# Per-part dependency buffers and measured step costs in the build-time order of a hybrid attention and gMLP layer

## What is computed

```python
h = x @ W_in + b_in                      # -> q | k | v | z | gate_a | gate_g
y_a = sliding_window_attention(q, k, v, sinks) @ w_br_a
y_g = chunked_spatial_gating(gelu(z), ...) @ w_br_g
mix = sigmoid(gate_a) * y_a + sigmoid(gate_g) * y_g
x = layer_norm(alpha * x + mix @ w_out)
x = layer_norm(alpha * x + relu(x @ w_up)**2 @ w_down)
```

## Time and profile before

| | |
|---|---|
| executions | 1038.11, 1037.97 and 1236.2 us; median 1038.11 us |
| profiled execution | 1037.65 us |
| its span on the slowest core (core 4) | 1036.1 us; cores 1035.0 to 1036.1 us |
| TensorE busy | 1004.8 us, granted clock 0.996 of full |
| VectorE, ScalarE, GpSimd busy | 589.8, 380.6, 101.3 us |
| DMA | 98.85 MB, 95 GB/s |

### The profile page before, as it was taken

How to read it: one execution, slowest core, us unless ns; L and a number is a source line. 1 busy time by engine, 2 the same in 40 slices (tenths; PEclk the granted TensorE clock), 3 DMA queues, 4 the chain that set the end, 5 groups by cost and what they waited for, 6 DMA issues and landing times.

```text
span 1036.1 us, 16955 instructions; the slowest of 8 cores (1035.0 to 1036.1 us)
## 1 busy us (share of the span) xinstructions
PE 1004.8 (97%) x5792; PEld 491.3 (47%) x5902; DVE 589.8 (57%) x1226; ACT 380.6 (37%) x578; POOL 101.3 (10%) x163
## 2 busy tenths in 40 slices
PE   9999999999999999999999999999999999999995
PEld 3446455554444444444444645555444444444442
DVE  3866577765776312444676837777486842134454
ACT  0456566641325200331134645666223430023221
POOL 4210000000111000000023000000010100010015
PEclk9999999999999999999999999999999999999998
DMA  9995243253787902954299222632366564086012
GB/s 163 194 174 97 42 66 58 42 114 84 148 144 147 151 8 44 163 78 83 85 181 149 47 41 42 106 60 42 102 137 128 86 127 73 1 137 107 9 74 82
DMA packets 20630, 98.85 MB, mean 95 GB/s; under 512 B 2369, under 2 KB 3265, under 8 KB 12098
## 3 DMA queue, kind: packets, MB, share of 16 engines
q0 software_dynamic: 13200, 73.14, 45.2%
q1 hardware_dynamic: 7346, 24.61, 7.2%
HBM read 162.50 MB, written 8.39 MB: 165 GB/s over the span
## 4 chain that ended last, share of the span: by engine, by line
PE 90%; DVE 5%; issue 2%; ACT 1%; DVEq 0%; POOL 0%; ACTq 0%; POOLq 0%
PE ps L443 58%; PE ps L1206 21%; PE ps L696 3%; DVE scr L948 2%; PE ps L977 1%; PE ps L936 1%; PE ps L552 1%; ACT regK L415 1%; PE ps L836 1%; PE ps L998 1%; PE ps L1123 1%; PE ps L1029 1%; PE ps L1219 1%; DVE lnbuf L401 1%; DVE scr L404 1%
## 5 line engine op out<-in xcount | busy, mean ns | idle before, releaser
L443 PE MATMUL ps<-reg,ring 128*128 128x512 bf16 x1500 | 340.9, 379 | 2.4 <-issue 0.7
L443 PE MATMUL ps<-xT_s,ring 128*128 128x512 bf16 (+1 forms) x1060 | 245.6, 377 | 5.3 <-DVE den L1012 2.9
L443 PEld LDWEIGHTS ps<-reg,ring 128*128 128x128 bf16 x1536 | 147.4, 98 | 174.7 <-issue 3.9
L1206 PE MATMUL ps<-ring,reg 128*128 128x512 bf16 x972 | 213.7, 379 | 1.1
L415 ACT ACTIVATE scr<-ps 128x512 f32<-128x512 f32 x128 | 76.5, 597 | 262.8 <-PE ps L443 253.6
L443 PEld LDWEIGHTS ps<-xT_s,ring 128*128 128x128 bf16 x1104 | 103.1, 98 | 116.1 <-issue 6.8
L1206 PEld LDWEIGHTS ps<-ring,reg 128*128 128x128 bf16 x992 | 97.1, 98 | 117.0
L404 DVE SCALAR_TENSOR_TENSOR reg<-ps,scr 128x512 bf16<-128x512 f32 x128 | 87.7, 690 | 113.6 <-ACT scr L415 113.4
L948 DVE CUSTOM_DVE_ANT_1 scr<-ps,lnbuf 128x384 f32<-128x384 f32 x128 | 71.1, 555 | 51.2 <-PE ps L936 31.7
L415 ACT ACTIVATE scr<-scr,amx 128x384 bf16<-128x384 f32 x128 | 78.5, 613 | 37.1 <-DVE amx L404 30.0
L471 POOL DMA_DIRECT2D ring<-wst x62 | 34.2, 555 | 446.8 <-PE ps L443 177.3
(11 more groups left out here) (104 smaller groups left out, 824.3 us busy)
## 6 DMA issues: line engine op xcount, KB each, us to landing
ring<-wst POOLq DMA_DIRECT2D x62, 1024.0 KB, 10.5
regK<-x SPq DMA_DIRECT2D x16, 512.0 KB, 5.6
y<-scr SPq DMA_DIRECT2D x15, 512.0 KB, 3.0
lnbuf<-lnrep SPq DMA_DIRECT2D x4, 1024.0 KB, 9.4
xT_s<-xt POOLq DMA_DIRECT2D x2, 1024.0 KB, 20.9
ring<-wz POOLq DMA_DIRECT2D x2, 1024.0 KB, 10.4
xT_s<-xt POOLq DMA_DIRECT2D x7, 256.0 KB, 18.8
ring<-wz POOLq DMA_DIRECT2D x7, 256.0 KB, 14.9
```

The costliest lines, as they stand in the source:

```text
L443: r = e.matmul(out, lhsT=a, rhs=b, start=(k == 0), stop=(k == 7))
L1206: r = e.matmul(ps[:, b2 + half, :], lhsT=hreg[fi // 8][:, th, fi % 8, bb * 128:(bb + 1) * 128], rhs=wd[quarter][:, fi % 4, half * 512:(hal ...
```

## The change

The diff does three things.

1. Buffers by what is written. The maxima of attention get a buffer for each half of each unit (`B_mx`) and the negated ones a buffer for each unit (`B_nm`), the masked scores lie in two separate scratch slots by half, the two exponentials write two parts of one slot, and the statistics of the norms and the 8 groups of `Cg` get parts too. `parts` makes new buffers that come after all that used the old one.
2. Other costs in `schedule`, given as times of VectorE, ScalarE and single operations, a little other `seen_after`, and `own_after`: a delay between an operation and one that depends on it on the same engine.
3. `reads` and `writes` lists follow these buffers. No instruction is added, removed or resized; the place of the second half of the masked scores moves by 128 elements.

```diff
-        seen_after = {"pe": 0.3, "act": 0.2, "dve": 0.15, "pool": 0.2, "sp": 0.2}
+        seen_after = {"pe": 0.27, "act": 0.2, "dve": 0.2, "pool": 0.25, "sp": 0.2}
+        own_after = {"pe": 0.0, "act": 0.19, "dve": 0.185, "pool": 0.15, "sp": 0.0}
...
-                        at = max(at, t if d.dma else t if d.eng == e else t + seen_after[d.eng])
+                        at = max(at, t if d.dma else t + own_after[e] if d.eng == e else t + seen_after[d.eng])
...
-        B_amx = [Buf("amx%d" % i) for i in range(3)]
+        B_mx = [[[Buf("mx") for _ in range(2)] for _ in range(4)] for _ in range(3)]
+        B_nm = [[Buf("nm") for _ in range(4)] for _ in range(3)]
...
+        B_Cg = [Buf("Cg%d" % i) for i in range(8)]
...
         def dve_cost(ap):
-            return 0.17 + width(ap) / 940.0
+            return 0.075 + width(ap) / 950.0
+
+        def act_cost(ap):
+            return 0.105 if width(ap) <= 16 else 0.22 + width(ap) / 1430.0
+
+        def parts(n, after):
+
+            new = [Buf("part") for _ in range(n)]
+            Prog.alias_after(new, after)
+            return new
...
-                         0.28 + width(out) / 1120.0, tab)
+                         act_cost(out), tab)
...
-                o.alt = (lambda e: e.tensor_copy(out=out, in_=in_), 0.17 + width(out) / 1500.0)
+                o.alt = (lambda e: e.tensor_copy(out=out, in_=in_), 0.07 + width(out) / 1850.0)
...
+            hb = parts(2, [b])
             for h in halves:
-                timed(P.op("dve", (lambda h: lambda e: e.bn_stats(out=t[:, h * 6:h * 6 + 6], in_=src[:, h * 512:(h + 1) * 512]))(h), reads=R, writes=[b]), 0.79)
+                timed(P.op("dve", (lambda h: lambda e: e.bn_stats(out=t[:, h * 6:h * 6 + 6], in_=src[:, h * 512:(h + 1) * 512]))(h), reads=R, writes=[hb[h]]), 0.61)
...
-                mv = ms[:, 0:768].rearrange("p (s a n) -> p s a n", s=2, a=2)
+                mv = ms.rearrange("p (s r) -> p s r", s=2)[:, :, 0:384].rearrange("p s (a n) -> p s a n", a=2)
...
-                        reads=[B_ps[0], B_ps[1], C["masks"]], writes=[bms[0] if sub == 0 else bms[1], B_amx[ai]])
-                    o.cost = 0.65
+                        reads=[B_ps[0], B_ps[1], C["masks"]], writes=[bms[sub], B_mx[ai][bb][sub]])
+                    o.cost = 0.5
                 stt(mx[:, 8 + 2 * bb:10 + 2 * bb], mx[:, 2 * bb:2 * bb + 2], -0.125, negsk4[:, hk:hk + 1].broadcast_to([128, 2]), ALU.mult, ALU.min,
-                    [B_amx[ai], C["sinks"]], [B_amx[ai]])
-                pt, bpt = h1(4 + rot("P", 3))
+                    B_mx[ai][bb] + [C["sinks"]], [B_nm[ai][bb]])
+                pt, bslot = h1(4 + rot("P", 3))
+                bpt = parts(2, bslot)
...
-                    act(p16[:, :, sub * 192:(sub + 1) * 192], mv[:, sub], AF.Exp, bms + [B_amx[ai]], bpt,
-                        bias=mx[:, 8 + 2 * bb + sub:9 + 2 * bb + sub], scale=0.125)
-                cx[t].update(p16=p16, bpt=bpt)
+                    act(p16[:, :, sub * 192:(sub + 1) * 192], mv[:, sub], AF.Exp, [bms[sub], B_nm[ai][bb]], [bpt[sub]],
+                        bias=mx[:, 8 + 2 * bb + sub:9 + 2 * bb + sub], scale=0.125).cost = 0.52
+                cx[t].update(p16=p16, bpt=bpt + bslot)
...
-                P.op("dve", lambda e: e.reciprocal(out=d[:, 4:8], in_=d[:, 0:4]), reads=[B_den[di]], writes=[B_den[di]])
+                P.op("dve", lambda e: e.reciprocal(out=d[:, 4:8], in_=d[:, 0:4]), reads=[B_den[di]], writes=[B_den[di]]).cost = 0.1
...
-                             reads=[B_x1[blk], B_ps[b2], B_ps[b2 + 1]], writes=br2 + [bst]).cost = 1.35
+                             reads=[B_x1[blk], B_ps[b2], B_ps[b2 + 1]], writes=br2 + [bst]).cost = 1.16
...
-                                   reads=br2 + [bst], writes=bsqs + [bst]), 1.3)
+                                   reads=br2 + [bst], writes=bsqs + [bst]), 1.16)
```

More of the change, by code:

```diff
@@ L338, in build_program @@
         B_keep = [Buf("kk"), Buf("kv")]
-        C = {n: Buf(n) for n in ("bcol", "hgate", "brow", "ident", "sinks", "wsT", "tril", "Cg", "wsTb", "masks", "mhalf", "ones", "warm")}
+        C = {n: Buf(n) for n in ("bcol", "hgate", "brow", "ident", "sinks", "wsT", "tril", "wsTb", "masks", "mhalf", "ones", "warm")}
+        B_Cg = [Buf("Cg%d" % i) for i in range(8)]
         def h2(i):
@@ L410, in ts @@
             return timed(P.op("dve", lambda e: e.tensor_scalar(out=out, in0=in0, scalar1=s1, scalar2=s2, op0=op0, op1=op1), reads=R, writes=W),
-                         0.17 + width(out) / 1500.0)
+                         0.07 + width(out) / 1550.0)
         def act(out, in_, func, R, W, bias=0.0, scale=1.0):
@@ L421, in either @@
             o = timed(P.op("act", lambda e: e.activation(out=out, in_=in_, func=func, bias=b_, scale=1.0), reads=R, writes=W),
-                      0.28 + width(out) / 1120.0)
+                      act_cost(out))
             if bias is None:
-                o.alt = (lambda e: e.tensor_copy(out=out, in_=in_), 0.17 + width(out) / 1500.0)
+                o.alt = (lambda e: e.tensor_copy(out=out, in_=in_), 0.07 + width(out) / 1850.0)
             else:
@@ L429, in cp @@
         def cp(out, in_, R, W):
-            return timed(P.op("dve", lambda e: e.tensor_copy(out=out, in_=in_), reads=R, writes=W), 0.17 + width(out) / 1500.0)
+            return timed(P.op("dve", lambda e: e.tensor_copy(out=out, in_=in_), reads=R, writes=W), 0.07 + width(out) / 1550.0)
         def ld(dst, src, W, after=()):
@@ L584, in load_consts @@
             ld(idf, ident_d[:, :], [B_idf], after)
-            ld(Cg[:].rearrange("p g t -> p (g t)"), bs_d[:, :], [C["Cg"]], after)
+            ld(Cg[:].rearrange("p g t -> p (g t)"), bs_d[:, :], B_Cg, after)
         def load_masks(after=()):
@@ L610, in spatial_bias @@
                 stt(Cg[:, gi, :], ps[:, b + gi // 4, (gi % 4) * 128:(gi % 4 + 1) * 128], bcol[:, 40 + gi:41 + gi], Cg[:, gi, :],
-                    ALU.mult, ALU.add, [B_ps[b + gi // 4], C["bcol"], C["Cg"]], [C["Cg"]])
+                    ALU.mult, ALU.add, [B_ps[b + gi // 4], C["bcol"], B_Cg[gi]], [B_Cg[gi]])
         def prepare_sinks():
@@ L624, in ln_stats @@
             t, b = lst[:, s, :], B_st[s]
+            hb = parts(2, [b])
             for h in halves:
-                timed(P.op("dve", (lambda h: lambda e: e.bn_stats(out=t[:, h * 6:h * 6 + 6], in_=src[:, h * 512:(h + 1) * 512]))(h), reads=R, writes=[b]), 0.79)
+                timed(P.op("dve", (lambda h: lambda e: e.bn_stats(out=t[:, h * 6:h * 6 + 6], in_=src[:, h * 512:(h + 1) * 512]))(h), reads=R, writes=[hb[h]]), 0.61)
             if 1 in halves:
-                ahead(timed(P.op("dve", lambda e: e.bn_aggr(out=t[:, 12:14], in_=t[:, 0:12]), reads=[b], writes=[b]), 0.31))
+                ahead(timed(P.op("dve", lambda e: e.bn_aggr(out=t[:, 12:14], in_=t[:, 0:12]), reads=hb, writes=[b]), 0.13))
                 ahead(ts(t[:, 14:15], t[:, 13:14], eps, ALU.add, [b], [b]))
@@ L769, in spatial @@
                 stt(tq.rearrange("p (a t) -> p a t", a=4), ps[:, b, :].rearrange("p (a t) -> p a t", a=4), bcol[:, 32 + gi:33 + gi],
-                    Cg[:, gi, :].unsqueeze(1).broadcast_to([128, 4, 128]), ALU.mult, ALU.add, [B_ps[b], C["bcol"], C["Cg"]], btq)
+                    Cg[:, gi, :].unsqueeze(1).broadcast_to([128, 4, 128]), ALU.mult, ALU.add, [B_ps[b], C["bcol"], B_Cg[gi]], btq)
                 tt(sgT[:, th, gi, :], tq, uT[:, gi, th * 512:(th + 1) * 512], ALU.mult, btq + [B_uT[gi][th]], [B_sg[th]])
@@ L964, in att_S @@
                         out=bt[:, 0:16].rearrange("p (b j) -> p b j", b=8), in0=negsink[:, hk * 2:hk * 2 + 2].unsqueeze(1).broadcast_to([128, 8, 2]),
-                        in1=mx[:, 8:16].unsqueeze(2).broadcast_to([128, 8, 2]), op=ALU.subtract), reads=[B_amx[ai], C["sinks"]], writes=[B_bes[ai]])
+                        in1=mx[:, 8:16].unsqueeze(2).broadcast_to([128, 8, 2]), op=ALU.subtract), reads=B_nm[ai] + [C["sinks"]], writes=[B_bes[ai]])
                     act(bt[:, 16:32], bt[:, 0:16], AF.Exp, [B_bes[ai]], [B_bes[ai]], scale=-1.0)
@@ L1242, in d_A @@
                         bn = fin[:]
+                        fb = parts(4, [B_fin])
                         for ip, (c0, n) in enumerate(((0, 512), (512, 256), (768, 256))):
@@ L1250, in d_A @@
                                 ahead(timed(P.op("dve", (lambda i, c1: lambda e: e.bn_stats(out=bn[:, i * 6:i * 6 + 6], in_=r2[:, c1:c1 + 256]))(i, c1),
-                                                 reads=[br2[c0 // 512]], writes=[B_fin]), 0.45), 1.0 if ip else 0.4)
-                        ahead(timed(P.op("dve", lambda e: e.bn_aggr(out=t[:, 12:14], in_=bn), reads=[B_fin], writes=[B_st[sl]]), 0.31), 1.0)
+                                                 reads=[br2[c0 // 512]], writes=[fb[i]]), 0.35), 1.0 if ip else 0.4)
+                        ahead(timed(P.op("dve", lambda e: e.bn_aggr(out=t[:, 12:14], in_=bn), reads=fb, writes=[B_st[sl]]), 0.13), 1.0)
```

## The result

The changed kernel runs in 1025.03 us at the median, against 1038.1 us before. The ratio is 0.987, 95% interval 0.985 to 0.989, so it is 13 us or 1.3% faster. That is within the 2%, inside the range of 1022 to 1041 us, and the time that the forecast gave (1031.0) is 6 us too long.

What follows compares the result with a forecast made beforehand. TensorE, busy 97% of the span, was taken as the bound, with 31.3 us idle to win. From 1037.65 us, -2.6 - 2.5 - 0.5 - 1.5 = -7.1 gave 1030.5, and 0.46 for the median 1031.0 us; range 1022 to 1041.

Steps and rivals of the forecast that it cites:

- Part 1: Waits removed by the split buffers, chiefly in attention: -2.6 us, bounds 0 and -4.8.
- own wait: An operation's semaphore wait for an earlier one of its own engine, on VectorE or ScalarE: about 0.19 us on VectorE.
- rival 3: Waits on an engine's own instructions cost nothing, order stays: 1033.6 us, chance 0.05.
- 12 places: Attention score matmuls waiting for the masking of the unit before, each put 0.22 us shorter: -2.6 us.
- the wait at 168.25: In attention, scores following six transposes at 168.25 us of the timeline: TensorE was said to have stood 0.52 us.
- The bound of 4.8 us: Most that the removed waits could win: all twelve waits of attention scores for masking.
- The bound of 6.1 us: Most that splitting the norm statistics could give without matmul cover, 32 blocks at 0.19 us; forecast 0.
- Part 2: New planner order on all queues: -2.5 us from bank waits and -0.5 us from spatial matmuls.
- The four bank waits: In attention, dense matmuls waiting for a PSUM bank VectorE empties late, 2.9 us; put at -2.5 us.
- Part 3: After the last matmul, GpSimd's multiply goes before the last power operation, so VectorE isn't held: -1.5 us.
- rival 2: Attention waits nearly vanish: -11.5 - 1.8 - 1.5 = -14.8, so 1023.3 us, chance 0.15.
- rival 4: Slower: dense evacuations go ahead of masking, 0.4 us a place; 30 places give 1043 us, chance 0.16.

Runs made afterwards that it cites:

- e6: Changed kernel in the instruction order of the kernel before; only waits on an engine's own earlier instruction removed, those between engines put back: 1029.5 us, ratio 0.992.
- e7: Changed kernel, but the planner's delay between dependent neighbours on one engine (`own_after`) set to 0: 1037.5 us, ratio 0.999.
- e9: As e6, but only the 125 own waits in front of masking operations removed: 1032.9 us, ratio 0.995.
- e1: Changed kernel, but every engine runs its instructions in the order of the kernel before: 1031.8 us, ratio 0.993.
- e10: As e6, but only the 70 own waits of the norm statistics and `Cg` removed: 1036.3 us, ratio 0.998.
- e2: Changed kernel with split buffers, but all planner costs and delays of the kernel before: 1026.5 us, ratio 0.988.
- e3: Kernel before with only the new planner costs and delays, its buffers unsplit: 1027.0 us, ratio 0.989.
- e12: Changed kernel with one dependency more: block 6's last addition on VectorE waits for block 7's power operation on GpSimd; 1023.0 us, ratio 0.985.

## Why the prediction was right, and where it was off

**What bounds the kernel.** Right: all that was won lies in TensorE's idle time in attention, in the spatial matmuls ahead of it, and in the end. The idle time itself was misread, since core 4 lacks records: 8.3 us in the two windows in a core that has them all, not 11.5.

**Part 1, the price of an own wait.** Right: 0.19 us on VectorE, 0.22 behind the accumulator read, and about 0.2 on ScalarE (0.70 and 0.50 us between starts). The rule that the semaphore costs nothing (rival 3) falls twice: with the order fixed, cutting own waits gives 8.5 us (e6), and a planner that doesn't know them loses 14 us (e7).

**Part 1, what of it reaches TensorE.** This is the step that was mis-sized: 12 places x 0.22 us = 2.6 us, where masking's own waits gave 5.0 us (e9) and all removed waits 8.0 (e1). It took the saving at each wait as that of one own wait. At eight of the 12 places this is nearly right: one own wait of masking stands between VectorE's last idle moment (over 0.2 us) and the scores, and e9 gains 0.16 to 0.33 us there, 1.9 us together. The other 2.3 of the 4.3 us come from four places. At 631.1 us (core 1 of before) two own waits lie in that stretch and the gain is 0.46 us, their sum. At 127.9, 155.2 and 209.8 us one or none lies there, but VectorE also stood idle for 0.51, 0.37 and 0.49 us just ahead of it; in e9 this idle time is shorter or gone, and the gains are 0.78, 0.59 and 0.51 us. By what path removed waits shorten it is open. The rest of what the removed waits gave was put at nothing: other matmuls than the scores, the statistics, and the waits on ScalarE.

Two readings of the sum were off. The 0.22 us stand in 52 of the 64 units, not in all: in the others something lies between the halves already. And the wait at 168.25 cost 0.39 us, not 0.52: the undisturbed 0.33 us were taken with other matmuls behind the transposes, and with scores behind them it is 0.45 us (e1). The bound of 4.8 us was nearly right for the scores, which lost 5.3 us by their starts. The slack that was set against it, 36 us of idle VectorE in a window, says nothing of the moments in which TensorE waits.

**Part 1, the norm statistics at nothing.** Wrong: 2.1 us (e10). The cover named was the matmuls of the projections, but the spatial matmuls follow on the same VectorE with two banks, and of their 1.8 us in the earlier trace rows all but 0.4 were the lateness that the statistics left. The bound of 6.1 us held.

**Part 2, the order.** -3.0 us with the spatial matmuls were forecast. From e1 to the changed kernel it is 1016.2 - 1012.1 = 4.1 us. The four bank waits, chosen as likeliest to go, went, but they were 2.1 us and not 2.9. The reason given holds in e7: the planner must know what a chain costs. What it did not foresee is that either half of the change reaches nearly the same place alone (e2, e3).

**Part 3, the end.** -1.5 us forecast, 11.5 - 10.15 = 1.4 measured, by the named step: GpSimd's multiply ahead of the power operation, no 2.75 us operation. That the two agree so well is partly luck. The multiply ended 0.8 us earlier behind the last PSUM addition than was reckoned, and the last addition of two SBUF tensors (1.2 us) ran ahead of the four operations instead of behind them. Against that the power operation was held in its turn, which was not seen and is 0.6 us by e12, and 4.1 us instead of 3.6 lie between the last operation and the end of the span.

**The rivals.** The time came out nearer to rival 2 (1023.3 us, attention waits nearly vanish) than to the forecast, and its mechanism is what the trace shows. Its terms are near as well: by the stretches 10.3 us were won in attention for its 11.5, 2.6 us ahead of it for its 1.8, and 1.4 us at the end for its 1.5. (The 10.3 us are more than the 8.3 us of idle time that core 1 shows, since modelled ends hide a part of each wait.) The argument against it, "scores have two banks for all units, so each unit is tied to the one before", doesn't bind while masking is done in time. e7 has what rival 4 describes, 17 waits of the scores and 8.0 us, but from a planner that doesn't know the delay; whether dense operations stand ahead of masking there is not shown.

**Why the range held.** The parts of the forecast were 2.6, 3.0 and 1.5 us, the measured ones 8.0, 4.1 and 1.4. The range of 1022 to 1041 us was wide enough for a first part three times too small.

## What to carry to other kernels

When one engine is the bound and another one serves it in a chain, a cost per step on the serving engine is not sized by the one step in front of each wait of the bound engine: look at all steps since the serving engine last stood idle, at what that idle time itself hangs on, and at the other matmuls that the same engine serves. Fixing the order of all queues and removing the waits by kind gave the price here. Check too that the core whose idle time is read has all its records. Two instructions of one engine that share a dependency buffer without need cost about 0.19 us wherever they stand side by side, so give every separately written part its own. A planner at build time needs the delay between dependent neighbours at least as much as right durations: here durations 0.1 us too long did without it (e2), and right durations without it lost the whole gain (e7).

## What the runs showed of the hardware

An operation on one element a partition is held too. GpSimd's power operation took 0.55 us when it started before VectorE's addition of two SBUF tensors (e12) and 1.49 us when it started 0.14 us behind it (the changed kernel), ending 0.4 us after the 1.22 us addition did. In the earlier trace rows it was the other way round: VectorE's operation waited for GpSimd's. In both, the one that started first held the other. "SBUF — State Buffer" of the Trainium skill, section "SBUF: two separate sides", says that the shared pair is an exclusive lock and not a split of bandwidth, and that the one who starts first has it for the whole instruction, and these two cases agree.
